# Summing the squares of three RMS norms on GpSimd before one matmul with ones

## What is computed

```python
def rms_norm(x, g):
    y = x * rsqrt(mean(x * x, axis=-1) + EPS)
    return y * g

def modulate(x, g, shift, scale):
    return rms_norm(x, g) * (1 + scale) + shift

# layer 0: pooling mixer, then channel MLP; layer 1: gating mixer, then channel MLP
h = modulate(x, norm_g[i, 0], sh1, sc1);  x = x + g1 * mixer(h)
h = modulate(x, norm_g[i, 1], sh2, sc2);  x = x + g2 * (relu(h @ w1) ** 2 @ w2)
y = rms_norm(x, final_g)
# gating mixer (SGU): u, v = split(gelu(h @ w_in + b)); v = layer_norm(v)
#                     out = (u * (tril(W_s) v + b_s)) @ w_out      per chunk of 128 tokens
```

## Time and profile before

| | us |
|---|---|
| median of 3 runs | 1322.47 |
| lowest, highest | 1322.31, 1326.92 |
| the profiled execution, its time | 1323.73 |
| its span on the slowest core (core 3) | 1322.2 |
| spans of the eight cores | 1315.9 to 1322.2 |
| PE busy in the span | 1255.1 (95%) |
| DVE, ACT, POOL busy | 765.4 (58%), 587.5 (44%), 45.2 (3%) |

### The profile page before, as it was taken

How to read it: one execution, slowest core, us unless ns; L and a number is a source line. 1 busy time by engine, 2 the same in 40 slices (tenths; PEclk the granted TensorE clock), 3 DMA queues, 4 the chain that set the end, 5 groups by cost and what they waited for, 6 DMA issues and landing times.

```text
span 1322.2 us, 21660 instructions; the slowest of 8 cores (1315.9 to 1322.2 us)
## 1 busy us (share of the span) xinstructions
PE 1255.1 (95%) x7558; PEld 670.3 (51%) x7558; DVE 765.4 (58%) x1478; ACT 587.5 (44%) x1088; POOL 45.2 (3%) x87
## 2 busy tenths in 40 slices
PE   3299999999999999999999999999999999999995
PEld 0156565555555555555444444554545555554543
DVE  4287856545445454577657657854545445454567
ACT  5349443433333333466443555533333333333474
POOL 0001000000000000000000000000000000000000
PEclk9999999999999999999999999999999999999998
DMA  9999936434243342502000016511303031100024
GB/s 256 193 151 171 152 53 118 92 63 96 52 78 65 64 80 49 96 1 45 20 1 1 1 32 120 105 33 32 59 7 64 1 64 29 36 1 0 1 108 164
DMA packets 23880, 91.08 MB, mean 69 GB/s; under 512 B 2768, under 2 KB 10192, under 8 KB 15696
## 3 DMA queue, kind: packets, MB, share of 16 engines
q0 software_dynamic: 9392, 67.34, 28.7%
q1 hardware_dynamic: 14384, 22.35, 5.6%
HBM read 145.43 MB, written 11.01 MB: 118 GB/s over the span
## 4 chain that ended last, share of the span: by engine, by line
PE 89%; DMA 5%; ACT 2%; DVE 2%; issue 1%; POOL 0%; SPq 0%; DVEq 0%; ACTq 0%; POOLq 0%
PE ps L977 35%; PE ps L951 34%; PE ps L1126 5%; PE ps L1097 4%; PE ps L1213 4%; PE ps L793 2%; DMA ring<-w_pack 2%; PE ps L621 2%; DMA xT_sb<-x_pack 2%; ACT hT_sb L653 1%; PE ps L583 1%; PE ps L1128 1%; DVE xT_sb L1253 1%; DMA arena<-ln_b 1%; PE ps L1179 1%
## 5 line engine op out<-in xcount | busy, mean ns | idle before, releaser
L690 DVE SCALAR_TENSOR_TENSOR xT_sb<-ps,modT,xT_sb 128x512 f32<-128x512 f32 (+3 forms) x728 | 459.0, 638 | 440.5 <-PE ps L977 393.5
L977 PE MATMUL ps<-arena,ring 128*128 128x384 bf16 (+3 forms) x2624 | 521.7, 343 | 0.1
L951 PE MATMUL ps<-hT_sb,ring 128*128 128x384 bf16 (+2 forms) x2592 | 519.7, 345 | 0.0
L957 ACT ACTIVATE arena<-ps 128x384 bf16<-128x384 f32 (+3 forms) x324 | 169.6, 527 | 497.4 <-PE ps L951 497.3
L977 PEld LDWEIGHTS ps<-arena,ring 128*128 128x128 bf16 x2624 | 253.9, 98 | 215.6 <-issue 0.6
L951 PEld LDWEIGHTS ps<-hT_sb,ring 128*128 128x128 bf16 x2592 | 251.2, 98 | 216.2
L959 ACT ACTIVATE arena<-arena 128x384 bf16<-128x384 bf16 (+3 forms) x324 | 180.6, 561 | 28.8 <-ACT arena L957 2.2
L618 ACT ACTIVATE sq<-xT_sb 128x384 bf16<-128x384 f32 (+3 forms) x216 | 105.8, 530 | 72.1 <-DVE xT_sb L690 42.1
L643 DVE TENSOR_TENSOR hT_sb<-xT_sb,rstd 128x768 bf16<-128x768 f32 (+2 forms) x80 | 75.4, 1005 | 38.9 <-ACT rstd L635 38.8
L621 PE MATMUL ps<-sq,ones 128*128 128x384 bf16 (+3 forms) x216 | 49.0, 355 | 23.0 <-ACT sq L618 20.9
L1126 PE MATMUL ps<-ring,hT_sb 128*128 128x512 bf16 x272 | 67.2, 392 | 2.6 <-ACT arena L1102 2.6
(11 more groups left out here) (91 smaller groups left out, 467.6 us busy)
## 6 DMA issues: line engine op xcount, KB each, us to landing
ring<-w_pack POOLq DMA_DIRECT2D x62, 1024.0 KB, 9.0
xT_sb<-x_pack SPq DMA_DIRECT2D x3, 1536.0 KB, 21.6
xT_sb<-x_pack SPq DMA_DIRECT2D x2, 2048.0 KB, 18.9
y_pack<-xT_sb SPq DMA_DIRECT2D x8, 512.0 KB, 2.8
y_pack<-xT_sb SPq DMA_DIRECT2D x8, 384.0 KB, 2.5
ring<-w_pool POOLq DMA_DIRECT2D x1, 1024.0 KB, 24.1
y_pack<-xT_sb SPq DMA_DIRECT2D x4, 256.0 KB, 3.1
arena<-sp_pack POOLq DMA_DIRECT2D x1, 736.0 KB, 23.1
```

The lines of the kernel that those rows point to most:

```text
L690: nodes.append(S.op("dve", lambda e: e.scalar_tensor_tensor(out=xs, in0=P_(v)[:, 0:n], scalar=mcol(l, vG, dco), in1=xs, op0=ALU.mult, op1= ...
L951: mms = [(lambda e, dc=dc: e.matmul(P_(v)[:, 0:n], pv(key, 512)[:, dc, fc * 128:(fc + 1) * 128], hT.ap()[:, dc, c0:c0 + n], start=(dc == 0 ...
L957: ev = S.op("act", lambda e: e.activation(out=av, in_=P_(v)[:, 0:n], func=AF.Relu), reads=[(v.key, 0, 1)], writes=ak, cost=c_act(n), vbs=[v])
L977: mms.append((lambda e, fc=fc, av=av: e.matmul(P_(v)[:, 0:w], pv(key, 1024)[:, fc, dco * 128:(dco + 1) * 128], av, start=(fc == 0), stop=( ...
```

## The change

`stats` gets a second form, `summed`. ACT squares a channel block into a float32 tile of 512 columns; the memory of `sq` holds four of these in place of nine bfloat16 ones, and one of the four is the accumulator, which moves on by one from norm to norm. GpSimd adds the squares of the blocks 1 to 7 one after the other to the accumulator in float32, each add waiting for the one before it; the seventh writes its sum as bfloat16 to a tile of its own. PE then does a single matmul with ones. It is used for `norm(1, 0)` and `norm(1, 1)` in all five groups and for `final` in the four groups that are done in one piece: 14 groups, of which 8 have 384 columns and 6 have 512. The two norms of layer 0, and group 3 of `final`, keep eight matmuls. The scheduler gets a cost for GpSimd's adds and plans a new order.

```diff
+def c_pool(n):
+    return 0.2 + n * 0.0022
...
-    def stats(t0, n, own=False):
+    acc = [0]
+
+    def stats(t0, n, own=False, summed=False):
 
         v = S.vb("ps")
         mms = []
-        for dc in range(NDC):
+        if summed:
+            a = acc[0]
+            acc[0] = (a + 1) % 4
+            fs = [sqt.ap().bitcast(F32)[:, 512 * i:512 * i + n] for i in range(4)]
+            fk = [[("sq", 2048 * i, 2048 * i + 4 * n)] for i in range(4)]
+            ob, ok = sqt.ap()[:, 4096:4096 + n], [("sq", 8192, 8192 + 2 * n)]
+            for dc in range(NDC):
+                si = a if dc == 0 else (a + 1 + (dc - 1) % 3) % 4
+                S.op("act", lambda e, si=si, dc=dc: e.activation(out=fs[si], in_=xT.ap()[:, dc, t0:t0 + n], func=AF.Square),
+                     reads=XK(t0, t0 + n, [dc]), writes=fk[si], cost=c_act(n))
+                if dc:
+                    o, k = (fs[a], fk[a]) if dc < NDC - 1 else (ob, ok)
+                    S.op("pool", lambda e, si=si, o=o: e.tensor_tensor(out=o, in0=fs[a], in1=fs[si], op=ALU.add),
+                         reads=fk[a] + fk[si], writes=k, cost=c_pool(n))
+            mms.append((lambda e: e.matmul(P_(v)[:, 0:n], ones.ap(), ob, start=True, stop=True), ok + [("ones", 0, 1)], n))
+        for dc in range(NDC if not summed else 0):
...
     def norm(l, k, g):
         t0, n = GR[g]
-        R, RK = stats(t0, n)
+        R, RK = stats(t0, n, summed=True)
...
-        R, RK = stats(t0, n, own)
+        R, RK = stats(t0, n, own, summed=nn is None)
```

## The result

The changed kernel is slower, where the prediction had it faster.

| | us |
|---|---|
| before, median of 4 runs | 1323.26 (1322.31 to 1326.92) |
| after, median of 4 runs | 1336.78 (1335.61 to 1337.56) |
| ratio, 95% interval | 1.010 (1.0088 to 1.0112) |
| predicted | 1314.2 (1304 to 1331) |

The account below looks back on a forecast made before the run. The prediction took PE as the bound, holding 89% of the chain that ended last. Its terms, -18.2 + 2.6 + 3.9 + 3.4 = -8.3 us, took 1322.5 to 1314.2 us, range 1304 to 1331.

Parts of the forecast that it names:

- what stands beside them on DVE: In norm(1, 0) and final, adds in a row contend with DVE's z_ops and scales, delaying PE's ones matmuls: +3.4 us.
- the right mechanism among the rivals: GpSimd and DVE block each other in full, all 18.8 us reaching PE: 1318 to 1330 us, chance 0.28.
- Its strict reading: Contention rule for two-SBUF-input DVE instructions beside adds in norm(1, 0) and final, taken strictly: towards 18.8 us, not 3.4.
- The reserve of 1.7 us: Seven adds in a row, at 1.2 us each, were to end 1.7 us earlier than the planner assumed.
- Matmuls removed: Seven of eight ones matmuls go in 14 groups: 18.2 us less on PE, all in stretches the chain runs through.
- The gating mixer: PE's two waits behind norms of 512 columns in norm(1, 1) each grow by 1.3 us: +2.6 us.
- The end: Behind the last residual DVE has 29 scale instructions in the changed order, with six more to do there: +3.9 us.
- Slow adds: Rival: adds of 512 columns take 2.0 us, so ones matmuls come late: 1346 us, chance 0.14.
- the full gain: Rival: neither ACT's path nor DVE's end matters, so all 18.2 us are gained: 1304.3 us, chance 0.10.
- Squares to float32: ACT's squares write float32 in place of bfloat16, at no cost; a bfloat16 square of 512 columns took 623 ns.

Follow-up runs that it names:

- e7_plan: Changed kernel with the planner's cost of a GpSimd add raised from 1.33 to 2.04 us for 512 columns (1.04 to 1.65 for 384); 1325.41 us, ratio 1.0027.
- e5_psum_after: Changed kernel with rstd of its 14 norms left in PSUM, so z_ops and scales read one operand from SBUF; 1309.19 us, ratio 0.9899.
- e2_norm11: Kernel before with the summed form in norm(1, 1) only, eight matmuls kept in norm(1, 0) and final; two runs, 1322.20 and 1322.68 us.
- e12_due: Changed kernel with rstd in PSUM and the scales of final due 6 us late in the plan, not 30; 1310.53 us, ratio 0.9911.

## Why the prediction was wrong

**The sum's term that failed is "what stands beside them on DVE", +3.4 us.** With blocking (1336.8) and without (1309.2) the kernels differ by some 27 us, and by some 16 us where the plan charges more for the adds (e7_plan, 1325.4). Without this term the prediction's sum was 1322.5 - 11.7 = 1310.8 us, and e5_psum_after, in which it is close to zero, took 1309.2. That this is so near is partly luck: in e5_psum_after the stage of the two norms (299.5 us before, 286.6 there) gave 12.9 us and not 12.9 - 2.6 = 10.3, and `final` gave nothing where 5.3 - 3.9 = 1.4 us were expected. I had the right mechanism among the rivals, with its rule and its sign in the profile, and gave it 0.28 up to 1330; both the chance and the price were too low. The Trainium skill (SBUF — State Buffer, "Who interferes with whom") was set beside this term as the rule that speaks against the change, and the trace agrees with it: z_ops with two SBUF inputs are held up, 4.62 / 4 = 1.16 us to 8.24 / 4 = 2.06 us, and the residual of 512 columns (L711), which reads its other tensor from PSUM, is not (748 ns against 749). Its strict reading gave 18.8 us and was nearer than my half of it. Three things were missing even there:

- *Only the adds' lateness was priced, not DVE's.* z_ops that take 8.24 us in place of 4.62 push the residuals back, and these hold PSUM: the wait of 3.09 us for L711, and the late squares on which the next adds wait (5.31 us of GpSimd's idle time there, 4.06 us in the same place of e5_psum_after). I asked when PE gets its ones, and not what is queued behind the stretched instructions on DVE.
- *The reserve of 1.7 us did not exist.* It came from an add of 1.2 us. Measured are 1.27 us and 0.20 between dependent adds, a step of 1.47, against 1.45 planned. The estimate by the Trainium skill (GPSIMD Engine Reference, section 3.1), 1.33 us, was 0.06 us too high where mine was 0.07 us too low; that changes little by itself, but with the gap of 0.20 us, which neither had, it leaves no reserve.
- *A wait of PE costs more than its length.* 10.8 us of the changed kernel's loss is PE busy time, and some 8.8 of them are matmuls at a lower granted clock. It was to be seen before, too: eight matmuls of 512 columns behind the wait of 2.62 us took 3.32 us in place of 1.89, and I did not price it. (The clock of 0.92 in the last stretch of the earlier trace rows is not that: it is 1.00 up to 1309.70, and low only when PE has almost nothing left to do.) In e5_psum_after PE is busy for 1238.6 us, 16.5 less than before, so there nearly all of the 18.2 us came off.

**Matmuls removed, 18.2 us.** Right: 98 fewer, and 16.5 us less of PE where nothing is in the way.

**The gating mixer, +2.6 us.** The two waits named grew from 2.46 and 2.62 to 3.31 and 4.16 us, +2.4: right in place and size. The first now ends with DVE (L1218) and not with ACT's L1123, so its mechanism is not quite the one foretold. "The other three groups of norm(1, 1) show no such wait, and their gain stays" does not hold in e2_norm11: in the last group PE waited 1.34 us for squares in two waits before, and 2.49 us for adds there (1.54 in the changed kernel). In e5_psum_after the waits from 740 to 850 us come to 9.2 us, against 12.6 in e2_norm11. That this norm keeps its gain in e5_psum_after, where the same clock for the stages gives 286.6 us to the last output matmul in place of 299.5, and not in e2_norm11 (298.9), is not settled: no z_op was stretched in e2_norm11, so blocking is not what it lost there, and the orders of the two differ in many places.

**The end, +3.9 us.** As a row it came true: 1314.87 to 1327.76 is 12.9 us behind the last residual in place of 9.05. As a reason it was too narrow. e12_due, where 13 scales went back ahead of the last residual, ends no sooner. The order of the last rows is not what costs the 3.9 us; that DVE lacks time in the whole stretch is my reading, and not tested.

**Slow adds** (2.0 us) and **the full gain** (1304.3 us) fell: an add with DVE out of its way took 1.27 us, and the best kernel gets some 13 of the 18.2 us. **Squares to float32** are free, as predicted (627 ns against 623).

**The chances.** Slower had 0.16, most of it for slow adds. The point on which it turns was there to be worked out: 18.8 us of blocking against 11.7 us of gain leaves it 7 us slower by the prediction's own terms. Half of the price was taken on the argument that a held instruction meets the one in its way halfway on average. That may hold for two instructions that meet by chance, but not for two queues without gaps: there the rows show add and z_op each some 0.7 to 0.9 us longer, every time.

## What to carry to other kernels

Before arithmetic is moved to GpSimd, list what DVE does beside it and count the SBUF inputs of each instruction. Those with two were held up here and held up the adds in turn, and one form with a single one (the affine) was held up too. The price is the lateness of both queues and of all that stands behind either. Leaving the second operand in PSUM made such a pair free here (741 against 744 ns, and 27 us for the program). A matmul that waits for a serial chain needs the chain's step with its gap, and a wait of TensorE of some 3 us is to be priced with the lower clock behind it (1.4 us more for eight matmuls of 512 columns here).

## What the runs showed of the hardware

- GpSimd's float32 add with both inputs in SBUF takes 1.27 us for 128x512 and 1.00 us for 128x384 with DVE out of its way, 0.20 us between two dependent ones.
- Beside a z_op in two queues without gaps each pair takes 2.21 us, and neither engine is spared: the add goes from 1.27 to 2.01 us, the z_op from 4.62 / 4 = 1.16 to 2.06 us.
- An affine with only one tensor input (L677, bfloat16, 8 of 512 columns) is held up as well: 2.66 us with GpSimd idle, 4.01 us beside adds, and 3.93 us beside adds in e5_psum_after. The Trainium skill (SBUF — State Buffer, "Who interferes with whom") lists tensor_scalar among those that can take both port pairs, and these rows agree.
- A PSUM operand costs DVE nothing in these forms: 1216 against 1219 ns for 1024 columns of a z_op, 741 against 744 for a scale.
- Eight matmuls of 512 columns behind a wait of 3.34 us took 3.17 us from start to start at a granted clock of 0.54, where 1.73 us is their time at full clock.
